# A hybrid decoder step on one core: order of the compression rounds, and the block in which GpSimd issues its page loads

## What is computed

```python
def _compress(rows, w1, b1, w2, b2, pe):
    sub = rows[:, :n_sub * CMP_STRIDE].reshape(n, n_sub, CMP_STRIDE, NSA_KV_HEADS, HEAD_DIM)
    first = jnp.einsum('nspgd,pdh->nsgh', sub, w1[:CMP_STRIDE])
    second = jnp.einsum('nspgd,pdh->nsgh', sub, w1[CMP_STRIDE:])
    hid = first[:, :-1] + second[:, 1:] + (jnp.einsum('pd,pdh->h', pe, w1) + b1)
    return jnp.einsum('ncgh,hd->ncgd', jax.nn.gelu(hid), w2) + b2
```

## Time and profile before

| what | value |
|---|---|
| median of 3 runs | 1790.07 us (1789.44 to 1790.81) |
| the profiled execution's own time | 1790.02 us |
| its span, first to last instruction | 1788.3 us |
| PE busy | 1726.8 us, 97% of the span |
| DVE, ACT, POOL busy | 1027.8, 626.8, 335.7 us |
| mean granted clock of PE | 0.984 of full speed |
| DMA over the span | 178.16 MB, mean 100 GB/s |

### The profile page before, as it was taken

How to read it: one execution, slowest core, us unless ns; L and a number is a source line. 1 busy time by engine, 2 the same in 40 slices (tenths; PEclk the granted TensorE clock), 3 DMA queues, 4 the chain that set the end, 5 groups by cost and what they waited for, 6 DMA issues and landing times. The chain is left out here.

```text
span 1788.3 us, 30593 instructions
## 1 busy us (share of the span) xinstructions
PE 1726.8 (97%) x12640; PEld 1580.0 (88%) x12640; DVE 1027.8 (57%) x1875; ACT 626.8 (35%) x1277; POOL 335.7 (19%) x228
## 2 busy tenths in 40 slices
PE   8999999889999899999998999999999999999997
PEld 6889998457767669999887999999999999999996
DVE  6423130367787683352444469888888787533337
ACT  7421100278888622220333342322323332321211
POOL 0111200200000000000000025554555552322310
PEclk9999999789999999999999999999999999999998
DMA  5111738531102252110522321222222225422202
GB/s 205 39 58 41 244 102 265 186 110 60 58 8 94 74 162 72 48 36 25 235 108 106 96 89 61 72 85 83 73 72 84 75 93 199 155 96 96 96 24 98
DMA packets 70638, 178.16 MB, mean 100 GB/s; under 512 B 8733, under 2 KB 39645, under 8 KB 66941
## 3 DMA queue, kind: packets, MB, share of 16 engines
q1 hardware_dynamic: 65646, 170.97, 28.0%
q10 hardware_dynamic: 4088, 3.17, 0.6%
q0 software_dynamic: 768, 2.10, 0.4%
HBM read 148.91 MB, written 30.41 MB: 100 GB/s over the span
## 5 line engine op out<-in xcount | busy, mean ns | idle before, releaser
L2704 DVE TENSOR_TENSOR ff_sums_plain<-ps,ff_sums_plain 128x352 f32<-128x352 f32 x120 | 61.4, 522 | 117.8 <-PE ps L2251 117.4
L1287 ACT ACTIVATE big<-big 128x63 f32<-128x63 f32 (+8 forms) x192 | 114.1, 607 | 5.3 <-DVE big L1230 5.2
L2209 PE MATMUL ps<-ff_sums_high,mix_w_early 128*128 128x264 f32 x608 | 114.6, 285 | 0.5 <-DVE x L2603 0.5
L1530 PE MATMUL ps<-mix_x_high,out_w_high 128*128 128x352 f32 x384 | 108.7, 324 | 0.0
L1655 POOL MEMSET top<- 128x2048 f32 x1 | 1.8, 1805 | 530.4 <-POOLq L1368 530.4
L2209 PEld LDWEIGHTS ps<-ff_sums_high,mix_w_early 128*128 128x128 f32 x608 | 95.6, 188 | 0.7 <-DVE x L2603 0.7
L1530 PE MATMUL ps<-mix_x_high,out_w_low 128*128 128x352 f32 x288 | 93.0, 323 | 0.0
L2209 PE MATMUL ps<-ff_sums_high,ff_weights_high 128*128 128x264 f32 x304 | 87.3, 287 | 1.9 <-ACT x L2387 1.9
L2209 PE MATMUL ps<-ff_sums_low,ff_weights_high 128*128 128x264 f32 x304 | 87.3, 287 | 0.0
L2209 PE MATMUL ps<-ff_sums_high,ff_weights_low 128*128 128x264 f32 x304 | 87.1, 287 | 0.0
L2209 PE MATMUL ps<-ff_in_high,ff_weights_low 128*128 128x264 f32 x304 | 86.5, 284 | 0.0
(11 more groups left out here) (430 smaller groups left out, 5107.9 us busy)
## 6 DMA issues: line engine op xcount, KB each, us to landing
ff_weights<-in_w_up SPq DMA_DIRECT2D x22, 512.0 KB, 3.5
ff_weights<-in_w_gate SPq DMA_DIRECT2D x22, 512.0 KB, 3.6
ff_weights<-in_w_down SPq DMA_DIRECT2D x11, 1024.0 KB, 5.0
top<-in_mem_v SPq DMA_DIRECT2D x8, 1024.0 KB, 8.2
ff_in_plain<-activations_kept SPq DMA_DIRECT2D x12, 528.0 KB, 5.1
activations_kept<-ff_row SPq DMA_DIRECT2D x11, 528.0 KB, 2.6
activations_kept<-x SPq DMA_DIRECT2D x11, 528.0 KB, 2.7
ff_acts_plain<-activations_kept SPq DMA_DIRECT2D x10, 528.0 KB, 4.6
```

Of the source, the lines that this page charges most:

```text
L1287: nc.scalar.activation(s[:, x:y], s[:, x:y], ACT.Exp, bias=m[:, b:b + 1], scale=-1.0, accum_out=m[:, 8 + b:9 + b]).then_inc(exps, 1)
L1530: last = nc.tensor.matmul(K.bank[BANKS[n % 2][x]][:, 0:b - a], wt[:, n % 2, ws], h[:, a:b], start=k + m == 0, stop=k == KD - 1 and m == 2)
L2209: last = nc.tensor.matmul(K.bank[2 * slot + q][:, 0:QUART], wt[:, ws], xs[:, k, q * QUART:(q + 1) * QUART], start=opens and k + m == 0, st ...
L2704: nc.vector.tensor_tensor(XR[:, o, a:b], K.bank[(g * TILE + n) % 8][:, 0:b - a], XR[:, o, a:b], ALU.add).then_inc(down_taken, 1)
```

## The change

The list of rounds gets another order: both rounds of the second half come fourth and fifth, the prompt's v round last. POOL's gather moves from the sample attention into the compression block, behind a wait until `first` is 5, which is when PE has read all compressed pages of the second half. Everything else stays, ACT's issue after the fourth round too.

```diff
-    rounds = [(0, 0), (1, 0), (0, None), (1, None), (0, 1), (1, 1)]
+    rounds = [(0, 0), (1, 0), (0, None), (0, 1), (1, 1), (1, None)]
...
             sp.wait_ge(first, 2)
             gather(sp, K, 0, "sel")
 
+        @block.gpsimd
+        def _(pool):
+            pool.wait_ge(first, 5)
+            gather(pool, K, 1, "sel", 2, 2, own=True)
+
...
         @block.gpsimd
         def _(pool):
             nc.gpsimd.memset(qbd, 0.0).then_inc(zeroed, 1)
-            gather(pool, K, 1, "sel", 2, 2, own=True)
```

## The result

The changed kernel is slower: 1796.41 us median (1793.02 to 1797.88, 11 runs) against 1790.81 (1789.44 to 1792.8, 11 runs of the kernel before), a ratio of 1.0029 with a 95% interval of 1.0021 to 1.0038, that is 3.8 to 6.8 us. The forecast was 1797.5 (1794.3 to 1800.3). The profiled execution took 1797.87 us (span 1796.2), one of the slowest of the 11; it stands 7.85 above the profiled execution of before, so a comparison of the two traces has some 2 us more to account for than the medians have. Of these, 0.9 us is there before the change can act: the compression block's first matmul comes at 248.68 against 247.78.

The account below looks back on a forecast made before the run. It took PE, busy 97% of the span, as the bound. A block end 11.5 us later, less 3.0 for the wait and 1.0 for the clock, made +7.5 on 1790.02: 1797.5 us, range 1794.3 to 1800.3.

Parts of the forecast that it names:

- The block's end: Compression block's closing barrier: waits for POOL's issue and drain, so the block ends at 328.0, 11.5 us later.
- The issue: POOL's gather in the compression block: 12.9 us from start to drain, reaching its drain at 323.0, 6.5 us past the old end.
- The drain: POOL's drain ahead of the compression block's release: taken as 5.0 us, upper bound 6.35.
- The bound built from SP's row: Lower bound of POOL's drain, if its pages land as fast as SP's in quiet: 2.8 us.
- The page wait: PE's new fourth round waiting for the second half's compressed pages: 0.3 us, bounds 0 and 1.3.
- The wait of 3.04 us: PE's gap ahead of the second half's scores in the sample block: would go, -3.0 us.
- (d): Rival at the second half's scores: the wait stays because SP's last page is still late; +11.5, 1801.5 us; 4%.
- (c): Rival at the compression block's release: POOL doesn't decide the end, only the wait goes; -4.0, 1786.0 us; 4%.
- (b): Rival at the compression block's end: drain not paid, hold is the issue alone; +2.5, 1792.5 us; 4%.
- (a): Rival at the compression block's end: drain keeps its full 6.35 us, clock gives nothing; +9.9, 1799.9 us; 20%.
- The clock: PE at the second half's scores: may reach 2.4 GHz without the stop, a gain of 1.0 us, between 0 and 2.4.
- ACT's operands: ACT's sample operands after its fourth activation: issue moves from 285.2 to 297.4 to 295.7 to 307.9, nobody waits, cost nothing.

Follow-up runs that it names:

- e2: The changed kernel with the rounds in the old order, POOL's gather waiting for the sixth `first`: 1800.01 us against 1790.83 for the kernel before.
- e3: The changed kernel with only one of POOL's two sequences (8 pages) in the compression block, the other in the sample attention: 1789.74 us against 1790.83 before.
- e6: The changed kernel with POOL's pages back in the sample attention and 42 small clears in their place: 1802.64 us against 1791.51 for the kernel before.
- e10: Kernel before with new round order; in the compression block POOL issues 16 first-half pages, SP window keys and 8 second-half pages: 1786.80 us against 1790.83.
- e1: The kernel before with the new order of rounds alone, POOL's gather staying in the sample attention: 1790.95 us against 1790.83.
- e8: The changed kernel with SP's 16 second-half pages in the compression block as well: 1798.13 us against 1791.51 for the kernel before.
- e5: The kernel before with the second half's window keys (1 MB) loaded by SP at the compression block's end: 1788.37 us against 1791.51.
- e4: The kernel before with the new round order and SP's first 8 second-half pages issued in the compression block: 1791.50 us against 1790.83.
- e9: The kernel before with window keys loaded early and the memory's load issued after SP's 16 pages have landed: 1787.52 us against 1791.19.

## Why the prediction was right

Slower, inside the range, by the mechanism it named. Point by point:

- **The block's end.** "A block is over when its last engine is": shown by e2 (one for one), e3 and e6. The forecast had the block end 11.5 us later; between the traces it is 10.8 (327.3 against 316.5), of which 0.9 was there already at the compression block's first matmul (248.68 against 247.78) and has nothing to do with the change. So 9.9.
- **The issue.** 12.9 us from POOL's release to its drain was forecast from the place where it was seen; from `first` at 311.3 to 324.2 it is 12.9.
- **The drain.** Right as a term, and mis-sized: 5.0 taken, 3.1 measured. The step that failed is "nearer to POOL's own row than to SP's". The steadiness of POOL's landings in the earlier trace rows said nothing about an idle queue, since all of them fell in a loaded stretch. With little else under way POOL's pages land in 2.4 us, SP's in 2.2. The bound built from SP's row, 2.8, was nearly the value. The Trainium skill ("DMA: Bandwidth & Descriptors", the section on the anatomy of a DMA on the SWDGE path) gives 2.3 us for 128 KB by its fit; the landings of this kernel agree, 2.3 to 2.6, and the estimate of a 2.9 us drain that was worked out from it was better than mine. The upper bound was none either: beside SP's gather in e10 the drain is 9.9.
- **The page wait.** 0.3 taken, 0.66 in this trace, 0.40 in e1, 0.2 in e8, 0.81 in e6, none in e3 and e10; within its bounds. The new order alone is worth nothing by e1, as forecast.
- **The wait of 3.04 us** is gone, as forecast, and (d) with it. The hold and the drain are both there, which rules out (c) and (b); a drain near the 6.35 of (a) or above it is seen only where POOL's pages go out beside other loads (5.6 in e8, 9.9 in e10).
- **The clock.** 1.0 us was taken as a gain. The scores gave back 1.9 (5.7 to 3.8 us). But the stage's opening, from its first matmul to the wide biases of the second half, took 16.4 us instead of 15.5, at a granted 0.50 up to 335.7, and the values took 3.4 instead of 2.0. In this trace these parts together took about 0.6 us. Only the first of these was in the sum; the second was in its bounds; nothing in the text looked as far as the values. Their part isn't shown to come of the change: they took 3.0 us in e1, where only the order differs, and 2.0 in e3, which has a stop ahead of the stage. Nor is the opening's: it took 14.9 us in e2, behind a longer stop.
- **ACT's operands** went out from 297.1 to 309.0 and nobody waited for them.

The terms as measured, 9.9 for the hold, -3.1 for the wait (from the wide biases to the scores, 6.8 us became 3.7) and +0.6 for the clock, make +7.4 against the forecast's +7.5. That the two agree is luck: the hold was taken 1.6 us too long, and the clock was taken as a gain of 1.0 where this trace has a loss of 0.6. With the 0.9 that was there before they make 8.3 (366.28 to 374.57 at the first matmul behind the stage), of which the rest of the kernel took back 0.4: the profiled difference of 7.85. The difference of the medians is 5.6. The profiled execution was at the slow end of its kernel's runs, which differ in their mean granted clock (0.981 to 0.986); whether what is missing besides the 0.9 lies in the clock was not traced.

## What to carry to other kernels

An engine's list that is moved into another block is also work ahead of that block's barrier: add up its issue and its drain from its earliest possible start, and compare that with what the others still have to do. Here 16 us of POOL against 6 us of PE, ACT and DVE. Where the trace shows an engine waiting on a loaded stretch of DMA, look for any transfer whose place is free earlier and whose issue has nobody behind it: one DMA (e5) brought 3 us, where the move of sixteen lost 5.6. An early issue that lies early in its block doesn't hold it (e10); whether e10 gains anything over e5 by it is open.

## What the runs showed of the hardware

POOL's drain waits for its DMAs, SP's does not. In six traces it ends 0.4 to 0.7 us after POOL's last page has landed: 2.5 us to land and a drain of 3.1 (the changed kernel, e2), 2.4 and 2.6 (e3), 5.0 and 5.6 (e8), 5.8 and 6.3 (the kernel before), 9.3 and 9.9 (e10); without DMAs it takes 41 ns (e6). SP's takes 7 ns with pages under way (e4, and e8 at 325.0, where its last page landed at 328.8), and 128 ns at most in the barriers looked at.

SP's last page of a loaded stretch lands 1.5 us behind the one before it, also with no other load issued after it (e9). Why stays open.
